# Four 512-column products in a run, then their four 256-column products: a new order on TensorE in the wide blocks

## The chip, the core and the metric

The kernel runs on one core of one Trainium2 chip. The core has five engines that run side by side and meet at semaphores: TensorE (PE in the profile; PEld is its weight load), VectorE (DVE), ScalarE (ACT), GpSimd (POOL) and SyncE (SP), which here issues the DMA transfers. The metric is the device time of one execution in microseconds; a kernel's figure is the median of its runs.

## What is computed

Two transformer blocks in float32 over 256 tokens of width 2048, the output of the first being the input of the second. The first has a modulated norm, latent attention and a gated delta rule side by side, and a gated feed-forward part; the second has a convolution group and a neighbourhood attention, and a feed-forward part with a squared ReLU. Most of the work is the product of the activations with the weight matrices:

```python
    p = h @ w_in[l]                                            # 2048 x 9296
    ...
    gate, up = jnp.split(h @ w_gate_up[l], 2, axis=-1)         # 2048 x 11264
    x = x + gt_f * ((jax.nn.silu(gate) * up) @ w_down[l])      # 5632 x 2048
    ...
    proj = h @ w_in[l]                                         # second block
    mix = jnp.concatenate([yc, ya], axis=-1) @ w_out[l]        # 2048 x 2048
    f = jnp.square(jax.nn.relu(h @ w_up[l])) @ w_down[l]       # 2048 x 8192 x 2048
```

## The kernel before

**Tiles and units.** The weights are read as 6848 tiles of 128x128. Eight tiles make a unit of 128x1024, which is one DMA transfer of 512 KB. SyncE loads a unit into one of five slots of `RAW`; ScalarE writes its rounded high part into `HI` (line 567); VectorE subtracts it from `RAW` and writes the remainder into `LO` (line 723). Both have type float32r. `HI` and `LO` hold three units (`NHL`), so ScalarE can write the high part of a unit only when TensorE is done with the last tile of the unit three before.

**Activations.** They stand transposed in `H1` and `H2`, 16 rows of 512 columns: columns 0 to 255 are the high part of the 256 tokens, columns 256 to 511 the low part.

**Three ways to multiply a tile.** A product keeps three of the four terms (high x high, high x low, low x high).
- Narrow (1280 tiles, lines 367 to 369): three products of 256 columns into the same 256 columns of the bank.
- Wide (4288 tiles, lines 360 to 365): one product of 512 columns with the high part of the weights ("long"), and one of 256 columns with the low part of the weights ("short") into the second half of the bank. The evacuation adds the two halves.
- Tokens (line 376 to 378): the activations are the weights of the array, and four tiles at a time stream as 512 columns.

**The order.** The program is written as one walk over all tiles, in which every engine writes down the steps that are its own. `blocks` (and `block`, with one output) goes through the input rows `k` of a block of outputs and calls `tile` for each tile. In a wide tile with an even row count `c` TensorE issues long, short (lines 364, 365); with an odd one short, long (361, 362). So within a block of one output the order is long, short, short, long, and then long again. `e.matmul` carries the waits of `tile`: on `lo[u]` (the low part of the unit is written, which comes after the high part), on the row of activations `need(toks, k)`, and on the bank for the first row. Waits for a count that the engine has already passed are left out.

**What stands between tiles.** Evacuations, norms, rotary steps and attention steps are generators that wait in a list with a due tile; `flush`, called after every second tile of a unit, takes those that are due, and writes their TensorE steps (mostly in float32) at that point. Since the order of the steps on an engine is fixed by this walk, it is the same in every run.

Of the kernel before, what the change touches and what calls it, by code (L numbers as in the profile page):

```python
# [6 lines left out]
NRAW, NEARLY, NHL = 5, 8, 3  # L7
LAG, EVLAG, AHEAD = 3, 4, 2
# [6 lines left out]
ROWS_AHEAD = 1  # L15
DIRECT = 16
HAND = 4
TAPS = (5, 10)
N_STORES = 8

# [66 lines left out]
class Walk:  # L87
# [11 lines left out]
    def do(self, step, sem, *a, n=1, **k):  # L99
        at = self.count.get(sem, 0)  # L100
        self.count[sem] = at + n
        if step in self.mine:
            self.mine[step](*a, **(dict(k, at=at) if n > 1 else k))
        return (sem, at + n)
# [11 lines left out]
    def later(self, gen, lag=0, gap=LAG):  # L116
        self.pending.append([self.tile + lag, gen, gap])
# [22 lines left out]
    def need(self, lst, i):  # L140
        while lst[i] is None:
            self.force()
        return lst[i]
# [59 lines left out]
def program(nc, xT, pos, cols_d, consts_d, wada, wst, bias_d, gain_d, out, log):  # L203
# [8 lines left out]
    with ctx:  # L212
        def sb(name, shape, dt=f32):
            return ctx.enter_context(nc.sbuf_tensor(name, shape, dt))

        RAW = sb("RAW", [128, NRAW, 1024])
        HI = sb("HI", [128, NHL, 1024], f32r)
        LO = sb("LO", [128, NHL, 1024], f32r)
# [19 lines left out]
        S = {n: ctx.enter_context(nc.semaphore("s_" + n)) for n in SIGNALS + LOADS}  # L238
# [114 lines left out]
        def tensor(e):  # L353
            q = Engine(e, S)

            def tile(u, i, bk, H, k, wide, second, first, last, lo, h, free):
                q.wait_ge(lo, h, free)
                hh = HI[:, u % NHL, i * 128:i * 128 + 128]
                ll = LO[:, u % NHL, i * 128:i * 128 + 128]
                if wide and second:  # L360
                    e.matmul(bk[:, 256:512], ll, H[:, k, 0:256], start=False, stop=False, skip_group_check=True)  # L361
                    e.matmul(bk[:, :], hh, H[:, k, :], start=False, stop=last, skip_group_check=True).then_inc(S["tile"], 1)  # L362
                elif wide:
                    e.matmul(bk[:, :], hh, H[:, k, :], start=first, stop=False, skip_group_check=True)  # L364
                    e.matmul(bk[:, 256:512], ll, H[:, k, 0:256], start=False, stop=last, skip_group_check=True).then_inc(S["tile"], 1)  # L365
                else:
                    e.matmul(bk[:, 0:256], hh, H[:, k, 0:256], start=first, stop=False, skip_group_check=True)  # L367
                    e.matmul(bk[:, 0:256], hh, H[:, k, 256:512], start=False, stop=False, skip_group_check=True)  # L368
                    e.matmul(bk[:, 0:256], ll, H[:, k, 0:256], start=False, stop=last, skip_group_check=True).then_inc(S["tile"], 1)  # L369

            def tile_tokens(u, i, bks, H, k, first, last, lo, h, free, at):
                q.wait_ge(lo, h, free)
# [165 lines left out]
            def conv_square_sum(bk, a, square, free):  # L538
                q.wait_ge(square, free)
                for j in range(a, a + 4):  # L540
                    r = e.matmul(bk[:, 0:256], cn("ones"), B1[:, j, :], start=(j == 0), stop=(j == 7))
                r.then_inc(S["cv_p"], 1)

            walk(dict(tile=tile, tile_tokens=tile_tokens, x_turn=x_turn, direct=direct, c_spread=c_spread, spin=spin, stat_add=stat_add, stat_sum=stat_sum, acc2_sum=acc2_sum, rope_turn=rope_turn, kpe_swap=kpe_swap, ba_turn=ba_turn,
                      cumulate=cumulate, row_sum=row_sum, spread=spread, g_spread=g_spread, g_heads=g_heads, g_turn=g_turn,
                      g_turn_mt=g_turn_mt, g_pair=g_pair, g_ws=g_ws, g_state=g_state, g_out=g_out, turn=turn,
                      mla_scores=mla_scores, mla_values=mla_values, norm_turn=norm_turn, na_scores=na_scores, na_values=na_values,
# [439 lines left out]
        def walk(mine, log=None):  # L987
            w = Walk(mine)
            do, load, later, need, now = w.do, w.load, w.later, w.need, w.now
# [21 lines left out]
            lo_tok, hi_tok, unit_pe = {}, {}, {}  # L1011
# [73 lines left out]
            def feed(u):  # L1085
                u = min(u, len(lin_at) - 1)
                for v in range(len(hi_tok), u + 1):
                    hi_part(v)
                while st["proc"] <= lin_at[u]:
                    proc_next()  # L1090
                v = len(hi_tok)
                if v <= u + 1 and v < len(lin_at) and st["load"] > lin_at[v] and (v < NHL or v - NHL in unit_pe):
                    hi_part(v)

            def blocks(H, toks, k0, wname, kbase, outs, order=None, wide=False, apart=0):
                ks = list(order or range(len(toks)))
                banks = []
                for g in range(len(outs)):
                    ring = lbank if g < 3 and (lbank.idle or len(mbank.idle) < 3) else mbank
                    bi, bk, fr = ring.get()  # L1100
                    banks.append(((ring, bi), bk, fr))
                for c, k in enumerate(ks):
                    for g, (n, evac) in enumerate(outs):
                        own, bk, fr = banks[g]
                        u, i = divmod(w.tile, 8)
                        w.tile += 1
                        if log is not None:
                            log.append((wname, kbase + k, n))
                        if i == 0:
                            feed(u)  # L1110
                        last = c == len(ks) - 1
                        tok = do("tile", "tile", u, i, bk, H, k0 + k, wide, c % 2 == 1, c == 0, last, lo_tok[u], need(toks, k), fr if c == 0 else None)
                        if last:
                            later(evac(bk, tok, own), EVLAG + apart * g)
                        if i == 7:
                            unit_pe[u] = tok
                            feed(u + AHEAD)
                            w.flush()
                            yield
                        elif i % 2 == 1:  # L1120
                            w.flush()
                if i != 7:
                    yield

            def block(H, toks, k0, wname, kbase, n, evac, order=None, wide=False):
                return blocks(H, toks, k0, wname, kbase, [(n, evac)], order, wide)
# [86 lines left out]
            k = do("c_sigmoid", "pre_a", tk_cols)  # L1213
# [19 lines left out]
            for i in range(4):  # L1233
                bi, bk, fr = mbank.get()
# [80 lines left out]
            for b in range(DIRECT // 2):  # L1315
                ring = lbank if lbank.idle else mbank
                bi, bk, fr = ring.get()
# [110 lines left out]
            def qkv_chain(ns):  # L1428
                def first(j):
                    i, t, fr = tv.get()  # L1430
                    return i, t, do("tap_first", "ev_a", t, B1[:, j, :], COLS["conv_w"][0] + 4 * j, [raw_tok[j], fr], cw_tok)
                js = [n - 9 for n in ns]
                ahead = None
                for c, j in enumerate(js):
                    while raw_tok[j] is None:
                        yield
                    i, t, a = ahead or first(j)
                    v = do("taps", "ev_v", t, B1[:, j, :], COLS["conv_w"][0] + 4 * j, a, n=3)
                    s1 = do("tanh", "ev_a", B1[:, j, :], t, 1.0, v)
                    ahead = first(js[c + 1]) if c < 11 and raw_tok[js[c + 1]] is not None else None  # L1440
                    yield
                    qkv_tok[j] = do("scaled", "ev_v", B1[:, j, :], B1[:, j, :], 1.0, t, add, mult, s1)
                    tv.release(i, qkv_tok[j])
                    yield
                if ns is Q03:
                    later(qkv_chain(Q47), 0, TAPS[1])

# [211 lines left out]
            for b, n in enumerate(FIRST):  # L1659
                own, bk, _ = held[b // 2]  # L1660
                later(ev_first(n)(bk[:, 256 * (b % 2):256 * (b % 2) + 256], done_tok[b | 1], (own, b % 2)))
            later(scalars(), 16, 14)
            later(l2norm(0), 64, 6)
            later(qkv_chain(Q03), 20, TAPS[0])
            later(gdn(), 96, HAND)
            for n in REST:
# [271 lines left out]
            def ev_yb(j):  # L1938
                def f(bk, tok, own):
# [7 lines left out]
                    tv.release(i, m_tok[j])  # L1947
                return f
            run(blocks(H2, gdn_tok, 8, "w_o_gdn", 0, [(j, ev_yb(j)) for j in range(5)]))
            for j in range(5, 16):  # L1950
                run(block(H2, gdn_tok, 8, "w_o_gdn", 0, j, ev_yb(j)))
# [4 lines left out]
            def ev_res(gate, ST, extra, wide):  # L1956
# [17 lines left out]
                return mk  # L1974
            ev = ev_res(2, ST, need(x2_tok, 0), False)
            run(blocks(H1, m_tok, 0, "w_o", 0, [(j, ev(j)) for j in range(5)]))
            for j in range(5, 16):
                run(block(H1, m_tok, 0, "w_o", 0, j, ev(j)))
# [497 lines left out]
            for g in range(4):  # L2476
                for m in range(2):
# [3 lines left out]
                    bi, bk, fr = ring.get()  # L2481
                    turned[m, g] = bk, do("x_turn", "at_p", bk, m, g, x_tok[4 * g + 3], fr)
            w.run_pending()
            k = do("total", "st_v", [sq_tok[m, g] for m in range(2) for g in range(4)])
# [5 lines left out]
            for m in range(2):  # L2490
                for g in range(4):
                    dst = YT[:, m, 512 * g:512 * g + 512]
                    bk, tk = turned[m, g]
                    k = do("scaled", "ev_v", dst, dst, NT[:, m:m + 1], bk[:, :], mult, add, [r, tk], t_tok[m, g])
# [7 lines left out]
        block_.vector(vector)  # L2502
        block_.gpsimd(gpsimd)
        block_.tensor(tensor)


# [75 lines left out]
```

## Time and profile before

| | us |
|---|---|
| median of three runs | 2758.27 |
| lowest and highest | 2757.26 and 2758.77 |
| span of the profiled execution, first to last instruction | 2755.3 |
| TensorE busy in it | 2684.6 |
| VectorE, ScalarE busy | 1931.7, 1315.8 |

The median stands 3.0 us above the span of the profiled execution; that execution's own time is given only as this span, so the rest (what lies before the first and after the last instruction, and the spread of the runs) is taken to be the same for the changed kernel. Matmuls are pipelined: a row's duration overlaps that of the next, so the cost of a matmul in a run is the distance from its start to the next start, and not the duration. Times are from the start of the span.

### The profile page before, as it was taken

How to read it: one execution, taken by the hardware profiler on the slowest of the kernel's cores; microseconds unless marked ns; L12 is line 12 of the kernel's file. 1: busy time of each engine (PE TensorE's matmuls, PEld its weight loads, DVE VectorE, ACT ScalarE, POOL GpSimd, SP SyncE). 2: the span in 40 equal slices, each digit the busy share in tenths (PEclk: the TensorE clock that was granted, in tenths of full speed). 3: DMA queues.
4: the chain of work that ended last, by engine and by line, in shares of the span. 5: the costliest groups of instructions: out<-in, count | busy, mean ns of one | idle time of the engine just before them, and what ended most of it. 6: DMA issues, size and time to landing. Idle time of an engine off the chain costs nothing.

```text
span 2755.3 us, 41005 instructions
## 1 busy us (share of the span) xinstructions
PE 2684.6 (97%) x16144; PEld 2379.1 (86%) x16144; DVE 1931.7 (70%) x2983; ACT 1315.8 (48%) x2063; POOL 144.1 (5%) x132
## 2 busy tenths in 40 slices
PE   8989999999999999999999999999999999999998
PEld 7768988888899888888888889998888888888887
DVE  6868766876896886655555688997667466575665
ACT  2175644433544544444444454467555444444443
POOL 0000000000002000000000080111100000000000
PEclk9989999999999999999999999999999999999999
DMA  9944346666896786555555555554545555555554
GB/s 386 409 142 154 107 163 219 223 214 219 283 327 239 247 298 213 189 191 188 187 191 190 185 181 177 180 171 138 172 154 190 192 191 191 191 190 193 191 191 146
DMA packets 158737, 565.19 MB, mean 205 GB/s; under 512 B 17616, under 2 KB 21840, under 8 KB 158416
## 3 DMA queue, kind: packets, MB, share of 16 engines
q1 hardware_dynamic: 158544, 562.56, 59.8%
q8 instruction: 128, 2.10, 0.3%
q14 instruction: 65, 0.53, 0.1%
HBM read 560.39 MB, written 2.10 MB: 204 GB/s over the span
## 4 chain that ended last, share of the span: by engine, by line
PE 85%; DVE 8%; ACT 3%; DMA 2%; issue 1%; POOL 0%; DVEq 0%; ACTq 0%; SPq 0%; POOLq 0%
PE BK L364 17%; PE BK L362 17%; PE BK L365 9%; PE BK L361 8%; PE BK L376 4%; PE BK L377 4%; PE BK L378 4%; PE BK L367 4%; PE BK L369 4%; PE BK L368 4%; DVE LO L723 2%; PE BK L389 2%; PE BK L474 2%; DVE B L936 1%; ACT HI L567 1%
## 5 line engine op out<-in xcount | busy, mean ns | idle before, releaser
L567 ACT ACTIVATE HI<-RAW 128x1024 fp32r<-128x1024 f32 x824 | 873.6, 1060 | 1168.5 <-PE BK L362 638.6
L723 DVE TENSOR_TENSOR LO<-RAW,HI 128x1024 fp32r<-128x1024 f32 x824 | 1012.0, 1229 | 381.2 <-ACT HI L567 380.2
L364 PE MATMUL BK<-H,HI 128*128 128x512 f32 x2160 | 869.2, 405 | 17.3 <-DVE LO L723 16.7
L362 PE MATMUL BK<-H,HI 128*128 128x512 f32 x2128 | 840.8, 397 | 0.0
L365 PE MATMUL BK<-H,LO 128*128 128x256 f32 x2160 | 601.5, 278 | 0.0
L361 PE MATMUL BK<-H,LO 128*128 128x256 f32 x2128 | 595.8, 280 | 0.2 <-DVE H L761 0.2
L361 PEld LDWEIGHTS BK<-H,LO 128*128 128x128 f32 x2128 | 401.4, 189 | 93.7 <-DVE H L761 0.6
L365 PEld LDWEIGHTS BK<-H,LO 128*128 128x128 f32 x2160 | 408.2, 189 | 84.9 <-issue 1.0
L364 PEld LDWEIGHTS BK<-H,HI 128*128 128x128 f32 x2160 | 411.5, 190 | 29.7 <-DVE LO L723 20.5
L362 PEld LDWEIGHTS BK<-H,HI 128*128 128x128 f32 x2128 | 400.9, 188 | 3.9
L367 PE MATMUL BK<-H,HI 128*128 128x256 f32 x1280 | 376.2, 294 | 7.9 <-DVE LO L723 6.8
L369 PE MATMUL BK<-H,LO 128*128 128x256 f32 x1280 | 361.9, 283 | 0.0
L368 PE MATMUL BK<-H,HI 128*128 128x256 f32 x1280 | 361.8, 283 | 0.0
L367 PEld LDWEIGHTS BK<-H,HI 128*128 128x128 f32 x1280 | 244.8, 191 | 13.0 <-DVE LO L723 9.6
L368 PEld LDWEIGHTS BK<-H,HI 128*128 128x128 f32 x1280 | 244.9, 191 | 1.5
L369 PEld LDWEIGHTS BK<-H,LO 128*128 128x128 f32 x1280 | 244.6, 191 | 0.0
L376 PE MATMUL BK<-HI,H 128*128 128x512 f32 x512 | 199.2, 389 | 0.0
L378 PE MATMUL BK<-HI,H 128*128 128x512 f32 x512 | 199.2, 389 | 0.0
L377 PE MATMUL BK<-LO,H 128*128 128x512 f32 x512 | 199.2, 389 | 0.0
L761 DVE TENSOR_TENSOR H<-TV,H 128x256 fp32r<-128x256 f32 x116 | 49.2, 425 | 163.7 <-ACT H L578 163.6
L378 PEld LDWEIGHTS BK<-HI,H 128*128 128x128 f32 x512 | 96.1, 188 | 20.2
L377 PEld LDWEIGHTS BK<-LO,H 128*128 128x128 f32 x512 | 96.1, 188 | 19.9
(267 smaller groups left out, 2541.1 us busy)
## 6 DMA issues: line engine op xcount, KB each, us to landing
RAW<-wst_dram SPq DMA_DIRECT2D x837, 512.0 KB, 3.4
RAW<-wada_dram SPq DMA_DIRECT2D x155, 512.0 KB, 4.6
EARLY<-wada_dram SPq DMA_DIRECT2D x37, 512.0 KB, 11.0
EARLY<-wst_dram SPq DMA_DIRECT2D x19, 512.0 KB, 12.2
X<-xT_dram SPq DMA_DIRECT2D x8, 512.0 KB, 7.2
B<-bias_dram SPq DMA_DIRECT2D x32, 128.0 KB, 3.4
out_dram<-B SPq DMA_DIRECT2D x8, 256.0 KB, 2.2
B<-gain_dram SPq DMA_DIRECT2D x1, 1024.0 KB, 4.8
```

Of the source, the lines that this page charges most:

```text
L361: e.matmul(bk[:, 256:512], ll, H[:, k, 0:256], start=False, stop=False, skip_group_check=True)
L362: e.matmul(bk[:, :], hh, H[:, k, :], start=False, stop=last, skip_group_check=True).then_inc(S["tile"], 1)
L364: e.matmul(bk[:, :], hh, H[:, k, :], start=first, stop=False, skip_group_check=True)
L365: e.matmul(bk[:, 256:512], ll, H[:, k, 0:256], start=False, stop=last, skip_group_check=True).then_inc(S["tile"], 1)
L367: e.matmul(bk[:, 0:256], hh, H[:, k, 0:256], start=first, stop=False, skip_group_check=True)
L368: e.matmul(bk[:, 0:256], hh, H[:, k, 256:512], start=False, stop=False, skip_group_check=True)
L369: e.matmul(bk[:, 0:256], ll, H[:, k, 0:256], start=False, stop=last, skip_group_check=True).then_inc(S["tile"], 1)
L376: e.matmul(bks[m][:, :], H[:, k, 128 * m:128 * m + 128], hh, start=first, stop=False, skip_group_check=True)
L377: e.matmul(bks[m][:, :], H[:, k, 128 * m:128 * m + 128], ll, start=False, stop=False, skip_group_check=True)
L378: r = e.matmul(bks[m][:, :], H[:, k, 256 + 128 * m:384 + 128 * m], hh, start=False, stop=last, skip_group_check=True)
L567: e.activation(HI[:, u % NHL, :], raw_at(slot), ACT.Copy).then_inc(S["hi"], 1)
L723: e.tensor_tensor(LO[:, u % NHL, :], raw_at(slot), HI[:, u % NHL, :].bitcast(f32), sub).then_inc(S["lo"], 1)
```

## The change

`tile` keeps only the narrow form. The wide one is split into two steps: `wide_hi` issues the long product and waits for the high part of the weights (`hi_tok[u]`), the activations and the bank; `wide_lo` issues the short one, waits for the low part of the unit and counts the tile. `blocks` issues the long product of each tile at once and keeps its short one in a list `second`; after four tiles of the unit (`SHORTS`), or at the end of the block, the list is issued. The number of products, of loads and of evacuations is the same.

```diff
+SHORTS = 4
...
+            def wide_hi(u, i, bk, H, k, first, hi, h, free):
+                q.wait_ge(hi, h, free)
+                e.matmul(bk[:, :], HI[:, u % NHL, i * 128:i * 128 + 128], H[:, k, :], start=first, stop=False, skip_group_check=True)
+
+            def wide_lo(u, i, bk, H, k, last, lo):
+                q.wait_ge(lo)
+                e.matmul(bk[:, 256:512], LO[:, u % NHL, i * 128:i * 128 + 128], H[:, k, 0:256], start=False, stop=last, skip_group_check=True).then_inc(S["tile"], 1)
...
-                        tok = do("tile", "tile", u, i, bk, H, k0 + k, wide, c % 2 == 1, c == 0, last, lo_tok[u], need(toks, k), fr if c == 0 else None)
-                        if last:
-                            later(evac(bk, tok, own), EVLAG + apart * g)
+                        if wide:
+                            do("wide_hi", "tile", u, i, bk, H, k0 + k, c == 0, hi_tok[u], need(toks, k), fr if c == 0 else None, n=0)
+                            second.append((i, g, bk, own, evac, k0 + k, last))
+                            if i % SHORTS == SHORTS - 1 or (last and g == len(outs) - 1):
+                                for i2, g2, bk2, own2, evac2, k2, last2 in second:
+                                    tok = do("wide_lo", "tile", u, i2, bk2, H, k2, last2, lo_tok[u])
+                                    if last2:
+                                        later(evac2(bk2, tok, own2), EVLAG + apart * g2)
+                                second = []
+                        else:
+                            tok = do("tile", "tile", u, i, bk, H, k0 + k, c == 0, last, lo_tok[u], need(toks, k), fr if c == 0 else None)
+                            if last:
+                                later(evac(bk, tok, own), EVLAG + apart * g)
...
+                assert not second
```

On TensorE, a unit of the first wide blocks, in the kernel before (`BK1` is the bank, `s_lo` the semaphore of the low parts):

```order
L364 MATMUL BK1<-H1,HI 128x512 [waits s_lo]
L365 MATMUL BK1<-H1,LO 128x256
L361 MATMUL BK1<-H1,LO 128x256
L362 MATMUL BK1<-H1,HI 128x512
L364 MATMUL BK1<-H1,HI 128x512
L365 MATMUL BK1<-H1,LO 128x256
L361 MATMUL BK1<-H1,LO 128x256
L362 MATMUL BK1<-H1,HI 128x512
L404 MATMUL BK7<-SQ,CN 128x256 [waits s_ev_a,s_st_g]
L364 MATMUL BK1<-H1,HI 128x512
```

The same place on TensorE after the change:

```order
L367 MATMUL BK1<-H1,HI 128x512 [waits s_hi]
L367 MATMUL BK1<-H1,HI 128x512 x3
L371 MATMUL BK1<-H1,LO 128x256 [waits s_lo]
L371 MATMUL BK1<-H1,LO 128x256 x3
L406 MATMUL BK7<-SQ,CN 128x256 [waits s_ev_a,s_st_g]
L367 MATMUL BK1<-H1,HI 128x512 x4
```

The four long products now stand ahead of the wait for the low parts, which is on the first short one. Over the whole program the order shows 4482 places before and 2103 after at which a long and a short product of wide tiles stand next to each other (long before short or short before long); runs of less than four are left where a block ends inside a group or a float32 step stands in it.

On TensorE, the end of the first block of `w_down` in its third part, where the last two rows of activations (`s_ev_v`) come late, before:

```order
L362 MATMUL BK2<-H2,HI 128x512
L364 MATMUL BK2<-H2,HI 128x512 [waits s_ev_v]
L365 MATMUL BK2<-H2,LO 128x256
L361 MATMUL BK2<-H2,LO 128x256 [waits s_ev_v]
L362 MATMUL BK2<-H2,HI 128x512
L364 MATMUL BK0<-H2,HI 128x512
```

and after the change:

```order
L371 MATMUL BK2<-H2,LO 128x256 [waits s_lo]
L371 MATMUL BK2<-H2,LO 128x256 x3
L367 MATMUL BK2<-H2,HI 128x512 [waits s_ev_v] x2
L371 MATMUL BK2<-H2,LO 128x256 x2
L367 MATMUL BK0<-H2,HI 128x512 x2
```

The second row is now asked for one short product earlier. SyncE and GpSimd have the same order as before; on VectorE and ScalarE a few steps change places at the end of two blocks with several outputs.

## Rows read from the trace of the kernel before

**Rows 1.** The page: busy us (share), TensorE's clock in 40 slices, the last chain.

```profile
PE 2684.6 (97%) x16144; PEld 2379.1 (86%) x16144; DVE 1931.7 (70%) x2983; ACT 1315.8 (48%) x2063; POOL 144.1 (5%) x132
...
PEclk9989999999999999999999999999999999999999
...
PE 85%; DVE 8%; ACT 3%; DMA 2%; issue 1%; POOL 0%; DVEq 0%; ACTq 0%; SPq 0%; POOLq 0%
```

**Rows 2.** The page, wide products: busy time and mean ns, then idle time before.

```profile
L364 PE MATMUL BK<-H,HI 128*128 128x512 f32 x2160 | 869.2, 405 | 17.3 <-DVE LO L723 16.7
L362 PE MATMUL BK<-H,HI 128*128 128x512 f32 x2128 | 840.8, 397 | 0.0
```

**Rows 3.** Timeline of TensorE, a steady wide block: start us, duration us, instruction.

```profile
1000.16 0.39 PE L364 MATMUL BK<-H,HI 128*128 128x512 f32 x1
1000.40 0.28 PE L365 MATMUL BK<-H,LO 128*128 128x256 f32 x1
1000.51 0.28 PE L361 MATMUL BK<-H,LO 128*128 128x256 f32 x1
1000.63 0.40 PE L362 MATMUL BK<-H,HI 128*128 128x512 f32 x1
```

**Rows 4.** Stretches: length; busy (count) PE, PEld, DVE, ACT, POOL; clock; DMA; GB/s.

```profile
733.00:800.00 67.00, 61.45 (x466) 57.98 (x465) 63.15 (x112) 29.59 (x45) 0.00 (x0) 1.00 0.90 312
896.00:925.00 29.00, 25.83 (x134) 21.75 (x133) 27.14 (x48) 14.04 (x22) 0.00 (x0) 0.94 0.57 192
1000.00:1500.00 500.00, 500.00 (x2870) 436.17 (x2870) 307.19 (x411) 233.77 (x332) 0.00 (x0) 1.00 0.60 199
```

**Rows 5.** Timeline, five outputs at once: the first and the 81st matmul.

```profile
1944.75 0.40 PE L364 MATMUL BK<-H,HI 128*128 128x512 f32 x1
...
1958.74 0.40 PE L364 MATMUL BK<-H,HI 128*128 128x512 f32 x1
```

**Rows 6.** Timeline, only long products (token form): the first and the 44th.

```profile
2490.13 0.39 PE L377 MATMUL BK<-LO,H 128*128 128x512 f32 x1
...
2499.88 0.39 PE L378 MATMUL BK<-HI,H 128*128 128x512 f32 x1
```

**Rows 7.** Timeline, only short products (narrow form): the first and the 101st.

```profile
800.00 0.28 PE L369 MATMUL BK<-H,LO 128*128 128x256 f32 x1
...
811.99 0.28 PE L367 MATMUL BK<-H,HI 128*128 128x256 f32 x1
```

**Rows 8.** Waits over the span: who for whom, us, times, longest us.

```profile
PE BK L364 <- DVE LO L723: 16.7, 10, 6.2
```

**Rows 9.** Timeline, 174 to 180 us; in brackets the idle time and its releaser.

```profile
174.82 1.04 ACT L567 ACTIVATE HI<-RAW 128x1024 fp32r<-128x1024 f32 x1
...
179.24 0.79 PE L364 MATMUL BK<-H,HI 128*128 128x512 f32 x1 [4.19 <-DVE LO L723]
```

**Rows 10.** Timeline, 904 to 912 us.

```profile
904.21 1.04 ACT L567 ACTIVATE HI<-RAW 128x1024 fp32r<-128x1024 f32 x1
...
911.25 0.50 PE L364 MATMUL BK<-H,HI 128*128 128x512 f32 x1 [2.44 <-DVE LO L723]
```

**Rows 11.** Timeline, 936 to 940 us.

```profile
938.48 1.22 DVE L723 TENSOR_TENSOR LO<-RAW,HI 128x1024 fp32r<-128x1024 f32 x1
...
939.75 0.50 PE L364 MATMUL BK<-H,HI 128*128 128x512 f32 x1 [0.88 <-DVE LO L723]
```

**Rows 12.** Timeline, 1567 to 1569 us, the first block of the third part of `w_down`.

```profile
1568.40 0.39 PE L361 MATMUL BK<-H,LO 128*128 128x256 f32 x1 [0.24 <-DVE H L761]
```

**Rows 13.** Timeline, four other waits of L364 for the low part.

```profile
167.39 0.80 PE L364 MATMUL BK<-H,HI 128*128 128x512 f32 x1 [6.18 <-DVE LO L723]
...
735.06 0.50 PE L364 MATMUL BK<-H,HI 128*128 128x512 f32 x1 [0.83 <-DVE LO L723]
...
905.74 0.50 PE L364 MATMUL BK<-H,HI 128*128 128x512 f32 x1 [0.37 <-DVE LO L723]
...
916.24 0.50 PE L364 MATMUL BK<-H,HI 128*128 128x512 f32 x1 [0.36 <-DVE LO L723]
```

More of the change, by code:

```diff
@@ L354, in tensor, with tile @@
             q = Engine(e, S)
-            def tile(u, i, bk, H, k, wide, second, first, last, lo, h, free):
+            def tile(u, i, bk, H, k, first, last, lo, h, free):
                 q.wait_ge(lo, h, free)
@@ L359, in tile @@
                 ll = LO[:, u % NHL, i * 128:i * 128 + 128]
[L360 to L369, printed above, removed]
+                e.matmul(bk[:, 0:256], hh, H[:, k, 0:256], start=first, stop=False, skip_group_check=True)
+                e.matmul(bk[:, 0:256], hh, H[:, k, 256:512], start=False, stop=False, skip_group_check=True)
+                e.matmul(bk[:, 0:256], ll, H[:, k, 0:256], start=False, stop=last, skip_group_check=True).then_inc(S["tile"], 1)
+            def wide_hi(u, i, bk, H, k, first, hi, h, free):
[4 more added lines that the diff above has]
+                e.matmul(bk[:, 256:512], LO[:, u % NHL, i * 128:i * 128 + 128], H[:, k, 0:256], start=False, stop=last, skip_group_check=True).then_inc(S["tile"], 1)
             def tile_tokens(u, i, bks, H, k, first, last, lo, h, free, at):
@@ L542, in conv_square_sum @@
                 r.then_inc(S["cv_p"], 1)
-            walk(dict(tile=tile, tile_tokens=tile_tokens, x_turn=x_turn, direct=direct, c_spread=c_spread, spin=spin, stat_add=stat_add, stat_sum=stat_sum, acc2_sum=acc2_sum, rope_turn=rope_turn, kpe_swap=kpe_swap, ba_turn=ba_turn,
+            walk(dict(tile=tile, wide_hi=wide_hi, wide_lo=wide_lo, tile_tokens=tile_tokens, x_turn=x_turn, direct=direct, c_spread=c_spread, spin=spin, stat_add=stat_add, stat_sum=stat_sum, acc2_sum=acc2_sum, rope_turn=rope_turn, kpe_swap=kpe_swap, ba_turn=ba_turn,
                       cumulate=cumulate, row_sum=row_sum, spread=spread, g_spread=g_spread, g_heads=g_heads, g_turn=g_turn,
@@ L1111, in blocks @@
                         last = c == len(ks) - 1
-                        tok = do("tile", "tile", u, i, bk, H, k0 + k, wide, c % 2 == 1, c == 0, last, lo_tok[u], need(toks, k), fr if c == 0 else None)
-                        if last:
-                            later(evac(bk, tok, own), EVLAG + apart * g)
+                        if wide:
[6 more added lines that the diff above has]
+                                        later(evac2(bk2, tok, own2), EVLAG + apart * g2)
+                                second = []
+                        else:
+                            tok = do("tile", "tile", u, i, bk, H, k0 + k, c == 0, last, lo_tok[u], need(toks, k), fr if c == 0 else None)
+                            if last:
+                                later(evac(bk, tok, own), EVLAG + apart * g)
                         if i == 7:
```

## The prediction, made before the changed kernel ran

> **What bounds the kernel.** I read the page first: TensorE is busy 97% of the span, carries 85% of the chain that ended last, and has its full clock in nearly all of the 40 slices [rows 1]. The reader should see there that almost nothing but TensorE's own stream can move the end. Then the costliest groups: the wide products are the largest, and the only wait that counts ahead of them is that for the low part of the weights, 16.7 us in 10 waits [rows 2, 8]. Busy time cannot tell what the order costs, because the durations of pipelined matmuls overlap: a row of 0.39 us stands beside starts 0.24 us apart [rows 3]. So I read start-to-start distances in long stretches without idle time. Last I looked at each wait in the timeline: what else was written by then, and whether another engine would hold TensorE up a moment later anyway.
>
> **Part 1, the order itself.** Every wide tile is one long and one short product before and after; only the neighbours change. Four stretches give the price of neighbours. Long products alone: 43 distances from 2490.13 to 2499.88, 9.75 us, 226.7 ns each [rows 6]. Short ones alone: 100 distances from 800.00 to 811.99, 119.9 ns each [rows 7]. Their mean, with no change of length at all, is 173.3 ns a product. Long, short, short, long has one change of length for two products: 500 us for 2870 products, 174.2 ns, so 0.9 ns more, or 1.8 ns a change [rows 4]. Five outputs at once go long, short, long, short, nine changes in ten products: 80 distances from 1944.75 to 1958.74, 174.9 ns, 1.6 ns more, again 1.8 ns a change [rows 5]. Two mixtures with different numbers of changes give the same price, and the two pure runs are its zero. The rule that a change of length costs about 1.8 ns is therefore my reading of four rows, not something that one row shows.
>
> The order lists 4482 changes before and 2103 after, 2379 fewer: 2379 x 1.8 ns = 4.3 us gained. Nothing lies beside this: in these stretches TensorE has no idle time [rows 4], so every nanosecond is on the path. The bounds: runs of four long products of wide tiles stand nowhere in the trace. If they went at the pure rates with no cost at the changes that are left, the gain would be the whole excess of 0.9 ns on 8576 products, 7.7 us. If the order didn't matter, 0. If long products kept their distance and short ones fell back to the pure rate, it is a loss; that is the rival below. I take 4.3, because both mixtures lie on the line.
>
> By the Trainium skill ("TensorE: Matmul & The Clock Gate", section "Back-to-back issue gap") an isolated product of N columns takes N/2.4 + 2.5 ns, as an estimate 216 and 109 ns, whoever its neighbour is; by it Part 1 would be zero. The rows disagree on the size (226.7 and 119.9) and on the neighbours; they decide here, and what the rule would give stands first among the rivals.
>
> **Part 2, a wait that starts later in the stream.** The long products now wait for the high part only. Four of them take 4 x 0.233 = 0.93 us (0.233 is 2 x 174.2 ns less a short one at 0.115, the latter half of the 0.23 from 1000.40 to 1000.63 [rows 3, 4]). Before 179.24 TensorE waits 4.19 us for the low part, while the high part of that unit is written at 175.86 [rows 9]; before 911.25 it waits 2.44 us, and the high part is there since 905.25 [rows 10]. So up to 0.93 us of each such wait is filled. Of the ten waits, 16.7 us [rows 8], three are longer than that, 6.18, 4.19 and 2.44 us [rows 9, 10, 13]: they give 2.8 us. The other seven are 16.7 - 12.8 = 3.9 us together, the longest of them 0.88 [rows 11], and go wholly. The ceiling is 6.7 us.
>
> What is kept is less, since a gain ahead of a wait that another engine sets is lost in that wait. The first, at 167.39, is followed by the 4.19 us of rows 9, whose low part comes from a VectorE that isn't waiting for TensorE: take off 0.93. At 735.06 VectorE is busy 63.15 of 67 us and the DMA engines 0.90 of the stretch [rows 4, 13]: take off 0.83. The three waits at 905.74, 911.25 and 916.24 lie in a stretch in which VectorE is busy 27.14 of 29 us [rows 4, 10, 13], so the low parts come when they come, and only one filling of 0.93 is kept; the other two, 0.37 and 0.36, are taken off. Kept: 6.7 - 0.93 - 0.83 - 0.73 = 4.2 us. Bounds: 1.2, if VectorE's own chain also sets the waits of rows 11 and the short ones of the float32 stages, and 6.7. I take 4.2, for after each of the places that are left TensorE is soon busy without a gap again, as in the 500 us of rows 4.
>
> The clock dips where TensorE idles for microseconds; in the stretch of the wait before 911.25 its mean is 0.94 [rows 4]. That is 0.06 x 29 = 1.7 us of clock lost. Four long products run before the idle time instead of behind it, so such a dip can go, stay or turn up elsewhere: 1.7 us on each side of the sum, taken as zero.
>
> **Part 3, what is asked for earlier.** A long product needs its row of activations, and now stands ahead of up to three short ones that could have covered a late row: at most 3 x 0.12 = 0.35 us at each place. The trace has one such place, 0.24 us at 1568.40 [rows 12], and there the order shows one short product less of cover, 0.12 us; three more block starts of that kind show no wait. I take +0.3 us, bounds 0 and 1.4. Behind a waiting long product stand the short ones of its group, and behind these the count that ScalarE's next high part and the evacuations wait for; the last count of a unit comes where it came before, so nothing else starts later. The added waits, one for each of 536 wide units, are on products that already carry their weights' load; the wait for the low part at each unit's start costs nothing visible in a stretch of 500 us without idle time [rows 4], so I take them at nothing. If that cover were gone, each 10 ns would be 5.4 us. Nothing else moves: loads, evacuations, ScalarE and VectorE steps keep their order but for a few.
>
> **The sum.** -4.3 - 4.2 + 0.3 = -8.2 us. The profiled span of 2755.3 would be 2747.1; with the median 3.0 us above it as before, 2758.3 - 8.2 = **2750.1 us**.
>
> **Rivals.**
> - The order makes no difference: Part 1 is zero, the waits are as computed: 2758.3 - 4.2 + 0.3 = 2754.4 us. For it: long products in a mixture are only seen at two decimals one by one, and the excess of 0.9 ns might belong to the addresses or to the half of the bank that wide tiles use. Against it: rows 5.
> - The waits give nothing, because VectorE or ScalarE sets each of those places; the order gives its 4.3, and Part 3 takes 0.3: 2754.3 us. For it: VectorE's 27.14 of 29 us [rows 4]. Against it: TensorE is the busy engine right after 912 and 940 us.
> - **Slower.** In the mixture the short product goes at 0.115 us and the long at 0.233; alone at 0.120 and 0.227. If each long keeps 0.233 (because it is the wide form and not the neighbour that makes it so) and the shorts in a run fall to 0.120, a tile takes 353.3 instead of 348.4 ns: 4.9 x 4288 tiles = +21.0 us, less 3.9: 2775.4 us. It decides from the second short of a run on, in every group; break-even with Part 2 is at 0.9 ns a tile. Against it: the long's excess (6.6) and the short's lack (4.9) nearly cancel, as when a fixed time is only booked on the other side of a boundary.
> - More than computed: no cost at the changes left (7.7) and most of the ceiling of the waits (6): 2758.3 - 13.7 = 2744.6 us.
>
> That the change does not do what it says is excluded by the order, which lists the runs of four.
>
> **How the numbers follow.** The forecast, with 2747 to 2754 around it: 0.50. No difference by order 0.22. Waits give nothing 0.10. More than computed 0.09. Slower 0.09. A change of under 0.2% (5.5 us) is about what a measurement of this kernel cannot tell from none: faster means below 2752.8. Of the forecast's 0.50 some 0.41 lie there, with the 0.09 of the large gain and 0.02 of the first two rivals, whose own errors reach it: faster 0.52. What is left of these ends within it: 0.39. Slower: 0.09. The range of 8 in 10 leaves out the slower rival and half of the large gain, and goes 0.7 us over the time before, for waits that add up against it: 2744.5 to 2759.
>
> **What would show it.** In the changed profile: a stretch like that of rows 4 from 1000 to 1500 us with 173.7 ns a product, some 2878 instead of 2870 products (2870: the first rival; 2830: the slower one). Within a group long products 0.227 and short ones 0.120 us apart, but for the ones at a change. L367 without a wait for the low part, and on L371 a rest of about 16.7 - 6.7 = 10 us in three waits. No wait on the activations longer than 0.6 us. Wrong would be the whole reading if the distance of long products in a run of four stayed at 0.233 with short ones at 0.120, or if the second wait in a unit showed up as a gap in the middle of every unit.

## The result, and the profile after

The changed kernel takes 2762.07 us, the median of 16 runs (2760.24 to 2766.96); the kernel before took 2758.13 us in 16 runs beside them (2756.56 to 2760.47). The ratio is 1.0016, with a 95% interval of 1.0009 to 1.0023: 0.16% slower, 3.9 us. The forecast was 8.2 us faster, and the range ended at 2759.

The page of the changed kernel, the lines that answer to [rows 1]:

```profile
span 2763.0 us, 41005 instructions
...
PE 2693.1 (97%) x16144; PEld 2391.1 (87%) x16144; DVE 1929.5 (70%) x2983; ACT 1315.3 (48%) x2063; POOL 144.4 (5%) x132
...
PEclk9999999999999999999999999999999999999999
...
PE 85%; DVE 7%; ACT 4%; DMA 3%; issue 1%; SPq 0%; DVEq 0%; POOL 0%; ACTq 0%
```

The profiled execution took 2764.8 us by its own time, 2.7 us above the median of its kernel. Its span is 1.8 us less, as in most of the 16 runs, so the profiled execution of the kernel before, with 3.0 us between its span and the median, was about 1 us faster than that median. Both make the loss look larger by the spans (7.7 us) than by the medians (3.9). TensorE is busy for the same 97% and carries the same 85% of the last chain. Its busy time is 8.5 us longer (2693.1 and 2684.6), and what is left of the span is 0.8 us shorter: in this trace the loss isn't idle time.

A part of it is clock, which tenths of a slice don't show. The same two stretches, of the changed kernel first and of the kernel before below (the clock is the third number from the end):

```profile
355.00:359.00 4.00, 4.00 (x14) 3.38 (x15) 2.08 (x3) 2.19 (x7) 0.00 (x0) 0.57 0.47 146
1775.00:1779.00 4.00, 4.00 (x20) 3.89 (x21) 4.00 (x9) 2.45 (x6) 0.75 (x1) 0.57 0.54 119
```

```profile
355.00:359.00 4.00, 3.38 (x20) 2.88 (x20) 2.83 (x5) 3.13 (x11) 0.00 (x0) 1.00 0.27 76
1775.00:1779.00 4.00, 4.00 (x36) 4.00 (x35) 4.00 (x8) 2.56 (x5) 0.89 (x1) 1.00 0.42 130
```

In both stretches, and again at 772 us, the changed kernel's trace has 3.4 us at the lower level (1.2 GHz) that the trace before doesn't have. Before the first TensorE had only short waits (0.61, 0.29 and 0.62 us between 352 and 355 us, where the kernel before has the same ones and keeps its clock). A mean of 0.57 over 4 us is 1.7 us of full clock lost, as an estimate. Before 200 us the kernel before has more such time; over the span without its last microseconds it has 20.5 us at that level, 4.0 of them idle, and the changed kernel 23.9 and 2.9. Half of the difference in what isn't idle is 2.2 of the 7.7 us, as an estimate. Over all runs the mean granted clock differs little: 0.9951 in the changed kernel's 16, 0.9953 and 0.9956 in the 28 and 27 runs of the kernel before that were taken beside the experiments. Of the medians' 3.9 us that is at most 1.5, as an estimate.

The costliest wide groups and the waits for the low part, which answer to [rows 2] and [rows 8] (L367 is the long product, L371 the short one, L361 the first narrow one):

```profile
L367 PE MATMUL BK<-H,HI 128*128 128x512 f32 x4288 | 1202.4, 399 | 2.6 <-ACT HI L569 1.6
...
L371 PE MATMUL BK<-H,LO 128*128 128x256 f32 x4288 | 690.1, 282 | 11.7 <-DVE LO L725 11.7
```

```profile
PE BK L371 <- DVE LO L725: 11.7, 4, 5.5
...
PE BK L361 <- DVE LO L725: 6.7, 7, 1.8
```

Of the ten waits of wide products, 16.7 us, four with 11.7 us are left, and one of 1.6 us for the high part has come: the later wait did what it should. The loss is in the stretches without idle time. The stretch that answers to the last of [rows 4]:

```profile
1000.00:1500.00 500.00, 499.79 (x2849) 436.07 (x2848) 305.12 (x408) 231.85 (x330) 0.00 (x0) 1.00 0.59 198
```

2849 products in 500 us, 175.5 ns each, where it had been 2870 and 174.2. And the timeline in it, where equal instructions in a row are merged, so that the distance of two rows is that of a whole run:

```profile
1504.85 1.09 PE L367 MATMUL BK<-H,HI 128*128 128x512 f32 x4
1505.78 0.63 PE L371 MATMUL BK<-H,LO 128*128 128x256 f32 x4
1506.25 1.09 PE L367 MATMUL BK<-H,HI 128*128 128x512 f32 x4
```

Four long products take 0.93 us, or 0.232 each, hardly less than in the kernel before; four short ones take 0.47, or 0.118, where it had been 0.115.

I laid the two traces over each other by the number of tiles done. This table has what the kernel named is behind (+) or ahead of (-) the kernel before, in us, at that tile; the time is that of the kernel before. The columns after the first are experiments of the next section.

| tile | at us | changed | order only | runs of 2 | runs of 8 |
|---|---|---|---|---|---|
| 320 | 187.6 | -2.8 | -2.0 | -1.5 | -3.6 |
| 704 | 391.0 | +0.8 | +0.5 | -0.9 | +0.1 |
| 1344 | 719.8 | -0.8 | +0.7 | -1.7 | +6.7 |
| 1856 | 924.4 | -0.2 | +0.3 | -1.4 | +4.8 |
| 2112 | 1016.5 | -0.7 | +0.5 | -1.9 | +3.9 |
| 3648 | 1552.0 | +3.3 | +4.5 | -2.0 | +6.6 |
| 4416 | 1850.3 | +5.1 | +5.6 | -2.1 | +8.6 |
| 6720 | 2699.2 | +7.7 | +8.8 | -2.9 | +9.6 |

Each column compares two single executions, whose times differ by some microseconds from run to run, so a row shows a cause only where it stands out of that. By tile 320, after the two long waits, every kernel here is ahead, and those with the old wait as well: order only by 2.0 us, and the control with runs of two and the old wait, which has no column, by 1.9. Of the changed kernel's 2.8 us there, 0.8 is what the later wait may have given. From tile 2112 to 3648, a steady stretch, it loses 4.0 us in 1536 wide tiles, 2.6 ns a tile; the order-only kernel loses the same 4.0. From 3648 to 4416 the low clock at 1775 us is in the changed kernel's 1.8 us.

### The profile page after: what moved, and what is told of

It reads as the page before. It is cut to its first block, busy times and chain, and to the rows that moved or that the text cites. A ratio compares the mean times of both kernels' runs of the same rounds, so it can differ in the third digit from the quotient of the medians.

```text
span 2763.0 us, 41005 instructions
## 1 busy us (share of the span) xinstructions
PE 2693.1 (97%) x16144; PEld 2391.1 (87%) x16144; DVE 1929.5 (70%) x2983; ACT 1315.3 (48%) x2063; POOL 144.4 (5%) x132
## 4 chain that ended last, share of the span: by engine, by line
PE 85%; DVE 7%; ACT 4%; DMA 3%; issue 1%; SPq 0%; DVEq 0%; POOL 0%; ACTq 0%
PE BK L367 34%; PE BK L371 17%; PE BK L361 4%; PE BK L378 4%; PE BK L380 4%; PE BK L379 4%; PE BK L363 4%; PE BK L362 4%; DVE LO L725 2%; PE BK L476 2%; ACT HI L569 1%; DMA EARLY<-wada_dram 1%; PE BK L391 1%; DVE B L938 1%; DVE RAW L713 1%
## 5 line engine op out<-in xcount | busy, mean ns | idle before, releaser
L367 PE MATMUL BK<-H,HI 128*128 128x512 f32 x4288 | 1202.4, 399 | 2.6 <-ACT HI L569 1.6
L367 PEld LDWEIGHTS BK<-H,HI 128*128 128x128 f32 x4288 | 735.7, 190 | 102.8 <-issue 3.2
L371 PEld LDWEIGHTS BK<-H,LO 128*128 128x128 f32 x4288 | 662.7, 189 | 107.5 <-DVE LO L725 14.9
L371 PE MATMUL BK<-H,LO 128*128 128x256 f32 x4288 | 690.1, 282 | 11.7 <-DVE LO L725 11.7
L361 PE MATMUL BK<-H,HI 128*128 128x256 f32 x1280 | 377.2, 295 | 8.0 <-DVE LO L725 6.7
L363 PE MATMUL BK<-H,LO 128*128 128x256 f32 x1280 | 363.3, 284 | 0.0
L361 PEld LDWEIGHTS BK<-H,HI 128*128 128x128 f32 x1280 | 246.3, 192 | 12.4 <-DVE LO L725 9.3
L362 PEld LDWEIGHTS BK<-H,HI 128*128 128x128 f32 x1280 | 246.4, 192 | 1.1
L363 PEld LDWEIGHTS BK<-H,LO 128*128 128x128 f32 x1280 | 246.0, 192 | 0.0
L380 PEld LDWEIGHTS BK<-HI,H 128*128 128x128 f32 x512 | 96.1, 188 | 20.1
L378 PEld LDWEIGHTS BK<-HI,H 128*128 128x128 f32 x512 | 96.1, 188 | 19.8
L729 DVE TENSOR_TENSOR TV<-BK,TE 128x256 f32<-128x256 f32 x208 | 86.7, 417 | 36.8 <-ACT TE L573 36.6
L967 POOL TENSOR_TENSOR SQ<-SQ,B 128x256 f32<-128x256 f32 x49 | 61.2, 1249 | 943.1 <-ACT B L592 939.7
L938 DVE SCALAR_TENSOR_TENSOR B<-B,CO 128x256 f32<-128x256 f32 x240 | 108.2, 509 | 3.0 <-ACT B L656 2.9
## 6 DMA issues: line engine op xcount, KB each, us to landing
EARLY<-wst_dram SPq DMA_DIRECT2D x19, 512.0 KB, 12.2
```

The costliest lines, as they stand in the source:

```text
L367: e.matmul(bk[:, :], HI[:, u % NHL, i * 128:i * 128 + 128], H[:, k, :], start=first, stop=False, skip_group_check=True)
L371: e.matmul(bk[:, 256:512], LO[:, u % NHL, i * 128:i * 128 + 128], H[:, k, 0:256], start=False, stop=last, skip_group_check=True).then_inc( ...
L378: e.matmul(bks[m][:, :], H[:, k, 128 * m:128 * m + 128], hh, start=first, stop=False, skip_group_check=True)
L380: r = e.matmul(bks[m][:, :], H[:, k, 256 + 128 * m:384 + 128 * m], hh, start=False, stop=last, skip_group_check=True)
L729: e.tensor_tensor(dst, bk[:, 0:256], t, add).then_inc(S["ev_v"], 1)
L938: e.scalar_tensor_tensor(CA[j], UP[:, j, i:i + 256], CO[:, o + i:o + i + 1], CA[j], mult, add).then_inc(S["cv_v"], 1)
```

## Experiments

**The order without the later wait.** One wait goes back to where it was:

```diff
-  do("wide_hi", "tile", u, i, bk, H, k0 + k, c == 0, hi_tok[u], need(toks, k), fr if c == 0 else None, n=0)
+  do("wide_hi", "tile", u, i, bk, H, k0 + k, c == 0, lo_tok[u], need(toks, k), fr if c == 0 else None, n=0)
```

> The changed kernel's order, but the first long product of a unit waits for the low part of the weights as in the kernel before: the order alone, without the later wait. Theory now (a short product in a run of four stands 0.119 us from the next instead of 0.115, a long one 0.232 instead of 0.233): a wide tile takes 350.8 instead of 348.3 ns, +10.5 us against before, so 2768.5 us, some 6 us above the changed kernel; stretch 1010 to 1320 us at 175.3 ns a product. Rival A (the second wait in each unit costs the time, not the order): 2754 to 2758 us and 174.1 ns. Rival B (the later wait brings nothing, all of +4 is the order): 2762 us.

Measured: 2765.91 us, ratio 1.0026 (1.0017 to 1.0035). The stretch and the waits in its trace:

```profile
1000.00:1500.00 500.00, 499.36 (x2844) 435.48 (x2843) 304.63 (x407) 231.80 (x329) 0.00 (x0) 1.00 0.59 198
```

```profile
PE BK L367 <- DVE LO L725: 14.6, 9, 5.8
```

The distances are those of the changed kernel (175.4 ns from 1345 to 1560 us in both), though a unit has only one effective wait again. Expected were 2768.5 us, 2.6 more. So the order alone costs 7.7 us (2765.9 against 2758.2 beside it, with the same mean granted clock, 0.9954 and 0.9953), and the later wait gives back 2765.9 - 2762.1 = 3.8 us by medians of two measurements. Rival A, that the second wait costs the time, falls; so does rival B.

**Runs of two.**

```diff
-SHORTS = 4
+SHORTS = 2
```

> The changed kernel with runs of two: long, long, short, short. Both waits stay, one for the high and one for the low part in each unit. Theory (run length): shorts stand in pairs as before, so 174.1 ns a product and only the later wait is left, with 0.47 us of long products ahead of it instead of 0.93: gain of 3 to 4 us, 2754.5 us. Rival A (the second wait costs): 175.3 ns a product, about 2765 us. Rival from the prediction (1.8 ns a change of length, whatever the run): as many changes as before, 174.1 ns too.

Measured: 2754.51 us, ratio 0.9983 (0.9974 to 0.9992), as the run-length theory gave it; 174.1 ns a product from 1345 to 1560 us. The prediction's price of a change gives the same 174.1, so this run can't tell the two apart. It tells against the second wait as the cause: it has both waits in every unit, and as many increments as the changed kernel.

```profile
1000.00:1500.00 500.00, 500.00 (x2872) 436.15 (x2871) 308.36 (x412) 232.82 (x330) 0.00 (x0) 1.00 0.60 199
```

**Runs of one.**

```diff
-SHORTS = 4
+SHORTS = 1
```

> Runs of one: long, short, long, short in every wide tile. The price of a change of length (1.8 ns each, two a tile instead of one) says 174.9 ns a product, as in the five-output stretch of the kernel before: +0.7 ns x 8576 = +6 us, less 1 us of waits: 2763 us. Run length alone (shorts slow only in runs of three or more) says 174.1 ns and 2757 us.

Measured: 2769.61 us, ratio 1.0037 (1.0025 to 1.0049). Neither theory had it: 176.7 ns a product from 1345 to 1560 us. Its ten runs lie 17.2 us apart (2757.86 to 2775.08), those of every other kernel at most 7.5. And it is not one price. In the same trace, in blocks of one output, the same sequence runs at two speeds:

```profile
1005.16 0.28 PE L371 MATMUL BK<-H,LO 128*128 128x256 f32 x1
1005.27 0.39 PE L367 MATMUL BK<-H,HI 128*128 128x512 f32 x1
1005.50 0.28 PE L371 MATMUL BK<-H,LO 128*128 128x256 f32 x1
...
1006.20 0.28 PE L371 MATMUL BK<-H,LO 128*128 128x256 f32 x1
```

```profile
1504.95 0.28 PE L371 MATMUL BK<-H,LO 128*128 128x256 f32 x1
...
1506.01 0.28 PE L371 MATMUL BK<-H,LO 128*128 128x256 f32 x1
```

Three tiles take 1.04 us in the first stretch (0.347 each, and for some 60 tiles in a row), and 1.06 us in the second (0.353), where the long products repeat 241, 236, 233 ns. 0.347 is also the sum of the two settled distances, 226.7 and 119.9 [rows 6, 7], though here it is made up of 230 and 117. How much of a run goes at which speed isn't known for the other nine runs; shares that change from one execution to the next would give such a spread, which isn't shown.

**Runs of eight.**

```diff
-SHORTS = 4
+SHORTS = 8
```

> Runs of eight, a whole unit. Run length: shorts at 0.120 and longs at 0.232 within a run, about 352 ns a tile, 176.0 ns a product: +15.7 us of order against before, less 6 to 7 us of waits (1.86 us of long products ahead of the low part): 2767 us. If long products fall to 0.2267 once the run is long enough: 173.5 ns, 2747 us.

Measured: 2766.98 us, ratio 1.0032 (1.002 to 1.0043). The total is what the theory gave; the distances aren't (174.8 ns a product from 1345 to 1560 us, not 176.0), so it came out right for a wrong reason. The timeline:

```profile
1505.58 2.00 PE L367 MATMUL BK<-H,HI 128*128 128x512 f32 x8
1507.42 1.11 PE L371 MATMUL BK<-H,LO 128*128 128x256 f32 x8
1508.37 0.86 PE L367 MATMUL BK<-H,HI 128*128 128x512 f32 x3
```

Eight long products take 1.84 us (0.230 each) and eight short ones 0.95 (0.119). One by one, averaged over the 65 runs of eight, this trace shows the settling that I had not seen. The table gives the distance to the next start in ns, by place in the run, from 1345 to 1560 us:

| | 1st | 2nd | 3rd | 4th | 5th | 6th | 7th | 8th |
|---|---|---|---|---|---|---|---|---|
| long, run of 8 | 233.4 | 235.7 | 228.4 | 232.3 | 230.5 | 226.8 | 226.8 | 226.7 |
| long, run of 4 (changed kernel) | 234.1 | 234.5 | 231.7 | 228.6 | | | | |
| long, run of 2 (kernel before) | 232.9 | 233.4 | | | | | | |
| short, run of 8 | 113.4 | 119.1 | 120.0 | 120.0 | 119.9 | 120.0 | 120.0 | 120.0 |
| short, run of 4 (changed kernel) | 117.4 | 119.6 | 118.7 | 118.3 | | | | |
| short, run of 2 (kernel before) | 114.7 | 116.0 | | | | | | |

The place in the run isn't all: the first four of a run of four differ from the first four of a run of eight by up to 4 ns.

The rest of the loss of runs of eight lies elsewhere, and there it is idle time. TensorE is busy for 2684.3 us, as in the kernel before (2684.6), in a span 9.7 us longer; its trace is 6.7 us behind at tile 1344, in stages with float32 steps between the tiles. From 391 to 720 us the costliest wait there is that of a float32 step for a result of ScalarE, in runs of eight and, below, in the kernel before:

```profile
PE BK L476 <- ACT X L674: 6.9, 9, 1.2
```

```profile
PE BK L474 <- ACT X L672: 3.1, 9, 0.6
```

That this comes from the counts of eight tiles landing together, at the end of the unit, was not tried.

**The control: runs of two with the old wait.**

```diff
-SHORTS = 4
+SHORTS = 2
...
-  ... c == 0, hi_tok[u], need(toks, k), ...
+  ... c == 0, lo_tok[u], need(toks, k), ...
```

> Runs of two (long, long, short, short), with the first long product of a unit waiting for the low part as in the kernel before: the control for runs_of_2. Theory (run length sets the distances, the later wait gives the rest): 174.1 ns a product and the time of the kernel before, 2758.2 us within 1.5; the wait alone is then what runs_of_2 gained, 3.7 us. Rival (long, long, short, short is itself better than long, short, short, long): 2755 us here too.

Measured: 2757.05 us, ratio 0.9998 (0.9989 to 1.0007). Long, long, short, short is the kernel before, with its runs begun at another place. The later wait, with two long products ahead of it, is worth 2757.05 - 2754.51 = 2.5 us by medians of two measurements (the kernel before had 2758.0 beside the one and 2758.2 beside the other), where 3.7 was expected.

**The same addresses everywhere.** All wide products read activation row 0 and the first 128 columns of their unit's weights; the kernel leaves out the other rows and columns, and its output is another one. The bank that a product writes is not changed:

```diff
-  e.matmul(bk[:, :], HI[:, u % NHL, i * 128:i * 128 + 128], H[:, k, :], start=first, ...
+  e.matmul(bk[:, :], HI[:, u % NHL, 0:128], H[:, KEEP, :], start=first, ...
...
-  e.matmul(bk[:, 256:512], LO[:, u % NHL, i * 128:i * 128 + 128], H[:, k, 0:256], ...
+  e.matmul(bk[:, 256:512], LO[:, u % NHL, 0:128], H[:, KEEP, 0:256], ...
```

> The changed kernel's order, but every wide product reads activation row 0 and the first 128 weight columns of its unit, so its output is another one; the same number and length of products. If the distances in a run of four (233, 236, 228, 233 and 117, 120, 118, 117 ns) come from the addresses of rows or weights, they change: toward 226.7 and 120. If they come from the order of lengths alone, the eight distances and the 175.4 ns a product stay as they are.

Measured once (2759.94 us, beside 2758.04 for the kernel before): the distances in two runs of four from 1506.14 us on are 235, 234, 235, 225 and 117, 120, 120, 120 ns, and then 233, 236, 229, 232 and 118, 119, 117, 117, within 1 ns of those of the changed kernel at the same place. The stretch:

```profile
1000.00:1500.00 500.00, 499.79 (x2849) 436.10 (x2848) 305.50 (x408) 231.78 (x329) 0.00 (x0) 1.00 0.59 197
```

2849 products, to the number those of the changed kernel. The addresses of rows and weights don't set the distances. This execution has the order of the changed kernel without its low clock at 355 and 1775 us, and its span is 4.8 us shorter (2758.2).

**Long runs only where TensorE waits.** Runs of two, and runs of eight in the units where the low part comes microseconds late:

```diff
-SHORTS = 4
+SHORTS = 2
+LONG_RUNS = (*range(32, 42), *range(224, 240))
...
-                            if i % SHORTS == SHORTS - 1 or (last and g == len(outs) - 1):
+                            if i % (8 if u in LONG_RUNS else SHORTS) == (8 if u in LONG_RUNS else SHORTS) - 1 or (last and g == len(outs) - 1):
```

> Runs of two everywhere, but runs of eight in units 32 to 41 and 224 to 239, where TensorE waits microseconds for the low part of the weights. Theory: the steady stretches keep 174.1 ns; in the two stretches 1.86 instead of 0.47 us of long products stand ahead of the low part, and the runs-of-eight kernel gained 2.0 and 1.9 us more there than runs of two: 2754.5 - 3.9 = 2750.6 us. Rival (another engine's chain absorbs it later): 2754 us.

Measured: 2752.78 us, ratio 0.9982 (0.9974 to 0.9991). It is the fastest kernel here by its median. Its trace has less waiting than that of runs of two (12.2 us in 6 waits there):

```profile
PE BK L372 <- DVE LO L726: 9.0, 6, 4.2
```

The gain over runs of two is 1.7 us by medians of different measurements, less than half of the 3.9 expected; the intervals against the kernel before overlap nearly wholly, so that it is faster than runs of two isn't shown. Nor would the shorter waits be the only reason: the mean granted clock of its 11 runs is 0.9969, that of the runs-of-two kernel 0.9953 (runs of eight everywhere have 0.9968). Over 2750 us that is up to 4.4 us of full clock, as an estimate, of which idle time takes an unknown share.

**And runs of four at four short waits.**

```diff
+LONG_RUNS = {**dict.fromkeys((113, 137, 173, 568), 4), **dict.fromkeys((*range(32, 42), *range(224, 240)), 8)}
...
+                            if (i + 1) % LONG_RUNS.get(u, SHORTS) == 0 or (last and g == len(outs) - 1):
```

> As long_runs_at_waits, and runs of four in units 113, 137, 173 and 568, each of which has one short wait for the low part of 0.28 to 0.88 us. Theory: only waits above 0.47 us gain, two of them 0.4 us each, less 0.01 us of order: 2750.0 us. Rival: no difference from long_runs_at_waits that can be told, since VectorE sets the next wait.

Measured: 2753.58 us, ratio 0.9985 (0.9976 to 0.9994), 0.8 us above the kernel of long runs where 0.6 below it was expected (2750.0 against 2750.6). The rival holds: the two can't be told apart.

## Why the prediction was wrong

**Part 1 is the step that failed**, and within it the sentence "I take 4.3, because both mixtures lie on the line". Expected were -4.3 us; the order alone measured +7.7. Three things were wrong in it.

- The price of a change of length isn't a constant. Against the settled distances, a change costs (697.1 - 693.4) / 2 = 1.9 ns in runs of two, (1402.8 - 1386.8) / 2 = 8.0 in runs of four and (2792.9 - 2773.6) / 2 = 9.7 in runs of eight. In runs of eight the long products need five after a change to settle at 226.7, while the short ones are at 120 from the third on. A run of two ends while its short products still go at 115; a run of four reaches the slow short ones and stops before the fast long ones. The change halved the changes and made each four times as dear.
- The second point of the line was a mixture. The five-output stretch of [rows 5] switches between the two speeds of long, short, long, short that the runs-of-one trace shows apart (346.7 and 353.4 ns a tile), and its mean of 349.7 fell on the line by chance. In the trace before, three tiles of it take 1.04 us at first and 1.06 us soon after:

```profile
1952.10 0.39 PE L364 MATMUL BK<-H,HI 128*128 128x512 f32 x1
...
1953.14 0.39 PE L364 MATMUL BK<-H,HI 128*128 128x512 f32 x1
...
1955.22 0.39 PE L364 MATMUL BK<-H,HI 128*128 128x512 f32 x1
...
1956.28 0.40 PE L364 MATMUL BK<-H,HI 128*128 128x512 f32 x1
```

- The pure rates came from the middle of long runs [rows 6, 7]: they are right (runs of eight end on them), but no run of four gets there.

**The slower rival was the right one in kind, and twice too dear.** Its price was 4.9 ns a tile, with the long products at 0.233 and the short ones at 0.120; measured from 1345 to 1560 us are 232.2 and 118.5, 350.7 ns a tile, 2.2 more than the 348.5 of the runs of two there. It was given 0.09. Its argument against itself, that excess and lack cancel, holds in the runs of two only. The point from which it decides was put at 0.9 ns a tile, and the change is past it.

**Part 2 was right in size:** 4.2 us forecast, 3.8 measured as the difference of the two kernels that differ in this wait alone. That it is made up as the prediction has it isn't shown. The two traces end 1.1 us apart and not 3.8 (the changed kernel's is the one 2.7 us above its median). The waits of wide products for either part are 13.3 us in the changed trace and 14.6 in the order-only one. The prediction expected about 10 us in three waits for the low part and got 11.7 in four: the wait that was 0.36 us at 916.24 [rows 13] has become 1.93 at 915.25. What can be seen is the order of events: before tile 320 and around 911 us TensorE runs its four long products and then waits. In the changed trace:

```profile
907.02 1.09 PE L367 MATMUL BK<-H,HI 128*128 128x512 f32 x4
...
908.98 1.22 DVE L725 TENSOR_TENSOR LO<-RAW,HI 128x1024 fp32r<-128x1024 f32 x1
...
910.26 0.74 PE L371 MATMUL BK<-H,LO 128*128 128x256 f32 x4 [2.15 <-DVE LO L725]
```

The low part still comes when VectorE gets to it, as the prediction had it; and the wait of [rows 11] is gone. At the wait of [rows 9] the high part, too, is late, as its 175.86 us had implied, and that costs nothing, since the low part comes later still:

```profile
175.17 1.20 PE L367 MATMUL BK<-H,HI 128*128 128x512 f32 x4 [1.56 <-ACT HI L569]
...
178.49 1.22 PE L371 MATMUL BK<-H,LO 128*128 128x256 f32 x4 [2.12 <-DVE LO L725]
```

**Part 3 was right in size.** The row of activations of [rows 12] is waited for a little longer, 0.34 instead of 0.24 us:

```profile
1571.54 0.50 PE L367 MATMUL BK<-H,HI 128*128 128x512 f32 x1 [0.34 <-DVE H L763]
```

That the added waits are free is borne out: the order-only kernel, without an effective wait in the middle of the unit, has the same distances.

The dips of the clock, which the prediction took as zero with 1.7 us on each side, did turn up at other places, as told with the result, and the one at 355 us has no idle time of microseconds ahead of it. Between the medians the clock is worth at most 1.5 us, as an estimate.

**The other rivals fall.** The order does make a difference, the waits do give something, and nothing came of a larger gain.

**The numbers.** With the measured order in place of Part 1 the sum would have been +7.7 - 4.2 = +3.5 us, against the measured +3.9; Part 3 is within the 7.7, since the order-only kernel asks for the activations as early. The settled part can be followed: 2.2 to 2.6 ns on 4288 wide tiles are 9 to 11 us, as an estimate. The order-only kernel shows 7.7 by medians and 8.8 by its trace, which is 10.8 us from tile 320 on, with low clock at 355, 772 and 1775 us in it. The difference of 1 to 3 us between estimate and medians was not followed.

**The page and the rows.** The rows show 226.7 and 120 ns for settled products, and 224 to 241 and 112 to 121 around a change of length. The isolated gap of N/2.4 + 2.5 ns in the Trainium skill ("TensorE: Matmul & The Clock Gate", section "Back-to-back issue gap") gives 216 and 109, as an estimate, and knows no neighbours; measurement decides for these float32r products. The same section says that in a stream the spacing is set by the matmul and its weight load together, and gives about 131 ns for 512 columns; no product of 512 columns with a weight tile stands less than 223 ns ahead of the next in any trace here, and they settle at 226.7.

## What to carry to other kernels

A distance measured in a mixture of instructions holds for that mixture: before an order is changed, look in the trace for the new sequence itself at its new run length, and where there is none, price it from both sides and don't draw a line through two mixtures. A wait can be moved behind a few products for a gain that is the smaller of the wait and these products, less what the next wait of another engine takes back; here 3.8 us, in line with the sum. Where an order brings such a gain and costs issue time, it can be used only in the units that wait; that this beats short runs everywhere isn't shown here.

## What the runs showed of the hardware

- In alternating runs of eight, float32r products with a new weight load each settle at 226.7 ns (512 columns) and 120.0 ns (256 columns) only after five long or two short ones; before that, the averages are up to 236 for long ones and as little as 113 for short ones.
- Long, short, long, short has two steady speeds in one program, 346.7 and 353.4 ns a tile, each of which lasts for dozens to thousands of products. One stretch at the fast speed ended near 1027 us, and the slow one held from there to near 1574 us, for some 3090 products. What sets the speed stays open: both occur in blocks of one output, and addresses don't matter in runs of four.
- Neither a satisfied wait in the middle of a unit nor the addresses of the operands changed an averaged distance in the steady stretch by as much as 1 ns.
- With the same products and the same order, the places at which TensorE's clock falls to 1.2 GHz for 3.4 us differ from one execution to another: 355, 772, 915 and 1775 us in the changed kernel's trace, 770 and 910 us in that of the kernel with the same addresses.
